# Expert stage: the second matrix of each expert loaded through ScalarE's queue

## The reference

```
gates, idx = lax.top_k(affinity.transpose(0, 2, 1), cap)      # 16 experts, cap = 64 tokens
xin = h[bidx, idx]
hid = silu(einsum('becd,edf->becf', xin, w_gate)) * einsum('becd,edf->becf', xin, w_up)
y   = einsum('becf,efd->becd', hid, w_down) * gates[..., None]
out = zeros_like(h).at[bidx, idx].add(y)                       # D = 1024, f = 2048
```

## Time and profile before

| | us |
|---|---|
| median of 3 runs | 3158.36 |
| profiled execution | 3158.13 |
| its span | 3156.4 |
| TensorE busy | 2827.6 (90% of the span) |
| VectorE busy | 958.2 (30%) |
| ScalarE busy | 646.4 (20%) |
| GpSimd busy | 115.9 (4%) |

### The profile page before, as it was taken

The page is one execution under the profiler, slowest core; times in us unless marked ns, Lnnn a source line. Parts: engine busy times, 40 slices in busy tenths (PEclk is TensorE's granted clock), DMA queues, the critical chain, the costliest instruction groups (busy, mean ns, idle before and its releaser), DMA issues.

```text
span 3156.4 us, 39370 instructions
## 1 busy us (share of the span) xinstructions
PE 2827.6 (90%) x17108; PEld 1980.9 (63%) x17108; DVE 958.2 (30%) x1564; ACT 646.4 (20%) x1118; POOL 115.9 (4%) x125
## 2 busy tenths in 40 slices
PE   6987778599999999999979988999998988899997
PEld 3433553434333433433458857999998776799996
DVE  3026652311111111111162253423234243423323
ACT  1021441100100100010032142322223223321222
POOL 0000010000000000000000320000000050000000
PEclk8997889599999999999989869999999987999999
DMA  9234002199999999999911101223241110133321
GB/s 324 81 133 157 24 1 82 48 418 417 414 406 417 413 408 418 417 405 418 394 47 61 34 27 54 73 77 105 79 104 37 51 61 14 55 89 92 94 82 46
DMA packets 245291, 558.59 MB, mean 177 GB/s; under 512 B 36817, under 2 KB 198995, under 8 KB 220204
## 3 DMA queue, kind: packets, MB, share of 16 engines
q1 hardware_dynamic: 233584, 548.48, 45.6%
q0 software_dynamic: 1552, 5.70, 0.6%
q10 hardware_dynamic: 10028, 2.53, 0.4%
HBM read 552.46 MB, written 4.23 MB: 176 GB/s over the span
## 4 chain that ended last, share of the span: by engine, by line
PE 84%; DVE 10%; ACT 4%; issue 2%; DMA 0%; ACTq 0%; DVEq 0%; POOL 0%
PE vpsum L1825 20%; PE vpsum L1725 14%; PE apsum L1825 11%; PE vpsum L1742 7%; PE apsum L1709 4%; PE apsum L1834 3%; PE vpsum L1530 3%; PE vpsum L1767 2%; PE vpsum L1662 2%; PE apsum L1767 2%; PE apsum L1854 1%; PE apsum L1784 1%; PE vpsum L1967 1%; PE vpsum L1591 1%; PE vpsum L1605 1%
## 5 line engine op out<-in xcount | busy, mean ns | idle before, releaser
L1725 PE MATMUL vpsum<-ring,arena 128*64 128x512 f32 x2048 | 449.3, 597 | 0.8 <-ACT arena L839 0.8
L1825 PE MATMUL apsum<-stream_r,wring_r 128*128 128x264 f32 x2880 | 369.7, 289 | 15.9 <-DVE stream_r L1284 15.9
L1825 PEld LDWEIGHTS apsum<-stream_r,wring_r 128*128 128x128 f32 x2880 | 362.3, 193 | 19.1 <-issue 16.4
L1825 PE MATMUL vpsum<-work_r,wring_r 128*128 128x264 f32 x2880 | 353.7, 285 | 3.3 <-DVE work_r L1408 3.3
L1825 PEld LDWEIGHTS vpsum<-work_r,wring_r 128*128 128x128 f32 x2880 | 353.0, 189 | 3.4 <-issue 3.4
L1312 DVE TENSOR_TENSOR wring_r<-wring,wring_r 128x2048 fp32r<-128x2048 f32 (+3 forms) x100 | 207.2, 2076 | 407.1 <-ACT wring_r L879 407.1
L1725 PEld LDWEIGHTS vpsum<-ring,arena 128*64 128x64 f32 x2048 | 144.9, 138 | 291.3 <-issue 291.3
L1825 PE MATMUL vpsum<-stream_r,wring_r 128*128 128x264 f32 x2400 | 302.5, 286 | 10.5 <-DVE body L1395 10.5
L1825 PEld LDWEIGHTS vpsum<-stream_r,wring_r 128*128 128x128 f32 x2400 | 297.7, 191 | 10.9 <-DVE body L1395 10.9
L879 ACT ACTIVATE wring_r<-wring 128x2048 fp32r<-128x2048 f32 (+3 forms) x100 | 172.8, 1730 | 621.2 <-DMA wring<-w_ffn 600.9
L1742 PE MATMUL vpsum<-ring,arena 128*64 128x512 f32 x1024 | 226.8, 595 | 11.0 <-ACT arena L851 11.0
(11 more groups left out here) (394 smaller groups left out, 2707.2 us busy)
## 6 DMA issues: line engine op xcount, KB each, us to landing
ring<-w_gate SPq DMA_DIRECT2D x64, 2048.0 KB, 16.4
ring<-w_up SPq DMA_DIRECT2D x64, 2048.0 KB, 8.7
ring<-w_down SPq DMA_DIRECT2D x64, 2048.0 KB, 12.3
wring<-w_ffn SPq DMA_DIRECT2D x88, 512.0 KB, 4.7
ring<-w_ada SPq DMA_DIRECT2D x12, 2048.0 KB, 9.0
wring<-w_ffn SPq DMA_DIRECT2D x32, 704.0 KB, 4.6
ring<-w_in SPq DMA_DIRECT2D x5, 2048.0 KB, 23.2
wring<-w_in SPq DMA_DIRECT2D x10, 1024.0 KB, 5.4
```

Source lines behind the costliest of these rows:

```text
L1725: last = pe.matmul(banks[g][CAP * blk:CAP * blk + CAP, :], xin[:, 2 * r + c, :], w[:, at:at + 512], start=r + c == 0, stop=r + c == 4)
L1825: last = pe.matmul(b[:, k, 0:HW], w_[:, c, col:col + P], halves(x[:, c, :])[:, k, :].bitcast(FR), start=c == 0 and i == 0, stop=c == chunk ...
```

## The change

SyncE now issues only units 6 and 7 of the expert in work and units 0 to 5 of the next one. ScalarE issues units 8 to 11. Units 8 and 9 stand behind the first Silu of its loop, units 10 and 11 behind the second. The waits before each transfer, its semaphore, its slot and its source are those of before.

```
-                load_expert(e, range(6, 12))
+                load_expert(e, range(6, 8))
                 load_expert(e + 1, range(6))
-            load_expert(NE - 1, range(6, 12))
+            load_expert(NE - 1, range(6, 8))
...
                 for g in range(2):
                     act.wait_ge(gu_done, 8 * e + 4)
                     act.activation(sg[:, g, :], G_BANK[g][:, :], ACT.Silu).then_inc(silu_done, 1)
+                    for j in range(8 + 2 * g, 10 + 2 * g):
+                        src = expert_unit(act, e, j)
+                        act.wait_ge(gu_done, 8 * e + j - 6 + 1)
+                        act.dma_start(expert_slot(j), src).then_inc(loaded[(MOE_U + j) % NSLOT], 16)
                     if g == 0:
                         act.wait_ge(selT_done, e + 1)
                         act.activation(selT[:, 0, :], SELT_BANK[:, :], ACT.Copy).then_inc(selT_copied, 1)
```

## The result

The changed kernel takes 3187.58 us (median of 4 runs, 3178.26 to 3189.04), the kernel before 3158.34 us beside it. The ratio is 1.0081 (95% interval 1.0056 to 1.0105): slower, by 18 to 33 us. The forecast was 3161, that is, no change, in a range of 3156 to 3180: it was wrong. The profiled execution took 3178.26 us (span 3176.5, 20.1 more than before). It is the fastest of the four, so it shows less of the loss than the median.

A forecast was written before the change was run, and what follows sets the result against it. TensorE's own sequence was taken to bound the kernel. SyncE 0, ScalarE 0, 13 experts with slack 0 and three lagging ones 3 us, on 3158.1 of the profiled execution, gave 3161, range 3156 to 3180.

The forecast's parts named there:

- What bounds the kernel: Expert stage: TensorE's own sequence sets the 60.88 us period; weights arrive ahead, twelve units taking 58.7 us.
- SyncE's part: SyncE's queue: removing four issues of 0.33 us per expert makes nothing start earlier; gain 0.
- ScalarE's part: ScalarE's queue: four added issues, 1.6 us per expert, are covered since ScalarE arrives 8 us early; cost 0.
- my 0.4 us: ScalarE's queue: time assumed for each added issue with its address computations, four making 1.6 us per expert.
- Sharing by turns: Two queues alternate packet by packet, each getting half the bytes; unit 11's slack falls from 9.9 to 0.6 us; chance 0.50.
- Rival B: DMA queues: descriptors are served in order of issue, so nothing changes and lagging experts cost nothing; 3158, chance 0.18.
- Rival C: DMA engines stay with one queue for over a unit, making unit 11 0.5 us too late; 3169, chance 0.04.
- 0 (13 experts with slack) + 3 (three lagging ones): Waits on unit 11: none in 13 experts, 3 us together in three whose first unit landed late in the trace.
- 0.7 us of new idle time behind unit 7: DMA engines, per expert: idle time from unit 8's later issue, taken out of the 2.2 us gap at no cost.
- longer matmuls as a sign: TensorE: matmuls themselves taking longer than before would show the forecast wrong; no size given.
- Rival A: down(e, 1) waits for unit 11, from a start 0.3 us later on ScalarE's queue; 3177 to 3203, chance 0.25.
- Its milder case: down(e, 1): half of the extra start latency on ScalarE's queue, 0.8 us, costs 19 us in all; 3177.

The follow-up runs named there:

- units 0 and 1 held: Changed kernel, but SyncE issues the next expert's units 0 and 1 both at the eighth gu_done, unit 0 3.4 us later: 3160.99 us, ratio 1.0001.
- the two kernels with 8 KiB pieces: Changed kernel with 8 KiB instead of 16 KiB pieces, either for units 0 and 1 on SyncE's queue (3158.19 us) or for w_down on ScalarE's (3285.25 us).
- the one-queue kernel: Kernel before, all twelve units in SyncE's queue, but unit 8 waits for the fourth gu_done, 3.5 us later: 3160.83 us, ratio 0.9997.
- the kernel with the early unit 8: Changed kernel, but ScalarE issues unit 8 ahead of the first Silu, at the third gu_done: 3163.41 us, ratio 1.0003.
- the two profiles of the change: Changed kernel profiled at its first measurement (3187.58 us, ratio 1.0081) and when run once more unaltered (3193.06 us, ratio 1.0099).
- only 8, 9: Changed kernel, but ScalarE's queue loads only units 8 and 9, while 10 and 11 stay with SyncE: 3209.6 us, ratio 1.0151.
- 8 KiB on q10: Changed kernel, but w_down (units 8 to 11, ScalarE's queue) is read in 8 KiB pieces, units 0 to 7 in 16 KiB: 3285.25 us, ratio 1.0396.
- five-copy kernel: Kernel before, no transfer moved, but down(e, 1) waits while ScalarE copies the gathered tokens five times: 3247.27 us, ratio 1.0272.
- one-copy kernel: Kernel before, no transfer moved, but down(e, 1) waits until ScalarE has copied the gathered tokens once: 3180.48 us, ratio 1.0061.

## Why the prediction was wrong

**What bounds the kernel, and SyncE's part: right.** TensorE's chain set the pace, nothing was gained on SyncE.

**ScalarE's part: right in its cost, not in its issues.** The old waits of TensorE on ScalarE are the same to 0.1 us, and the queue ran ahead of Silu. The issues were less regular than my 0.4 us: units 8 and 9 took 1.27 us together in one expert above and 2.60 us in the other, and one issue alone took up to 2.1 us. The kernel with units 0 and 1 held has issues of up to 1.9 us and no loss, so they alone don't cost.

**Sharing by turns: right, and its number partly by luck.** I had unit 11 at 23.4 us after its issue with 0.6 us of slack; in an expert without a lag it took 23.2 us with 0.8 us. Two errors of opposite sign stand behind that. Unit 0 of the next expert took 14.2 us to land (issued at 959.8) where I had about 12, so the competition began later than I counted; and unit 9 landed 23.3 us after unit 6 was issued where I had 22.9, which counts double by unit 11. The rule itself is shown by the two kernels with 8 KiB pieces. Rival B (order of issue) is refuted by the packet counts. Rival C (long turns) is refuted by the first microsecond of the competition, in which each queue moved 15 packets: with turns of more than 8 packets per DMA engine, 4.9 us long, the second queue would have come in much more slowly.

**The step that failed: "0 (13 experts with slack) + 3 (three lagging ones)".** It was too small twice.

The count. I took the lags from the trace of before, three experts, as if the change left them alone. I had noted 0.7 us of new idle time behind unit 7 and charged nothing for it. With the late unit 8 lags are the rule: 14 experts in the one-queue kernel, 8 in the change, 3 in the kernel with the early unit 8. They meet a slack that was already spent, and what is late at unit 9 counts double at unit 11: over the 7 experts that waited in the first profile, 9.0 us of lateness at unit 9 (against 12.4 us to landing) became 19.4 us at unit 11 (against 23.2). In 6 of the 7 unit 6 was late; in the first expert of the stage only units 8 and 9 were. In the two profiles of the change 7 and 8 experts waited, 2.0 and 2.4 us each.

A stall also ends the lag. In the two profiles of the change, of the 14 experts that follow a stall of 1 us or more 2 have a late unit 6, and of the 16 that follow none 14 have. The kernels with a late unit 8 in which TensorE hardly waits for a transfer have 12 to 14 late ones; those in which it stalls in nearly every expert have 3 (only 8, 9) and 0 (8 KiB on q10). The kernel before with a wait of one copy, a period of 61.7 instead of 60.9 us, has none where it had 3. That fits DMA engines which need 58.7 of 60.9 us and catch up only when the period grows. Why a late issue of one unit sets the lag off is open: the one gap of 2.2 us became two, but no run shows what that does.

The price. I charged a stall its wait. Behind many stalls TensorE's granted clock is 0.5 as well, and the matmuls there take longer: 6.5 us on 14.1 in the first profile, 10.9 on 19.0 in the second, 34.5 on 52.5 in the five-copy kernel, which has no late transfer at all. The prediction had named longer matmuls as a sign that it was wrong, and gave them no term in the sum.

**Rival A was the outcome, by another way in.** It said `down(e, 1)` would wait for unit 11, which it does in 7 and 8 experts, but it asked for a later start on ScalarE's queue in every expert. Unit 8 was issued on time. Its milder case, 3177, came nearest; with the slow clock its own sum would have been higher.

**The range** ended at 3180 because the term of the lags had no upper bound of its own. Had each expert been given the lag of the worst three (2.2 us), 35 us would have stood there.

## What to carry to other kernels

Where the DMA engines are nearly full, as here (58.7 of 60.9 us), the order in one queue is a schedule: moving the transfers needed first to a second queue let later ones take half the bytes, and the size of the pieces set the shares. Bound the lateness of a transfer by its slack in every iteration, not by the lags seen while slack was plentiful. And price a stall of TensorE with the slow matmuls that may follow it: here they added 46% to 66% to the waits in the change and in the five-copy kernel, and 28% in the one-copy kernel.

## What was not expected of the hardware

Short waits of TensorE were often followed by a granted clock of 0.50. Counted over the profiles of all kernels here: behind each of the 51 waits of 2.3 us or more at `down`, its 32 matmuls took 8.4 to 10.1 us instead of 7.1. Of the 39 waits between 0.75 and 2.25 us, 10 were followed by such a slow `down` and 29 were not; the shortest with one was 0.76 us and the longest without one 2.2 us. Behind the wait of 1.2 us at L1767 the first four matmuls took 1.98 us and the next four 1.72, so nothing of that size was seen there. Two DMA queues moved near-equal counts of packets whether 16 KiB pieces met 16, 8 or 2 KiB ones, at a total rate (2 x 0.87 MB in 4 us of equal pieces, 435 GB/s) about that of one queue (429).
